# Attention's scores, a state space layer's matrices and skip, and the first unit of a stage, in another order

## The reference, cut to what matters

```python
for i in range(4):                    # attention, gating, state space, attention
    x = x + mixer_i(rmsnorm(x, norm_g[i, 0]))
    x = x + conv_gated_ffn(rmsnorm(x, norm_g[i, 1]), ...)
# attention: 16 heads of 64, instead of a softmax
z = q @ k.T / 8
log_1m = where(mask, log_sigmoid(-z), 0)
w = where(mask, exp(log_sigmoid(z) + cumsum_from_the_right(log_1m) - log_1m), 0)
o = (w @ v) @ w_o
# state space
bbar_re = coef_re * b_re - coef_im * b_im ; bbar_im = coef_re * b_im + coef_im * b_re
y = C x (a complex scan over time of bbar u) + d_skip * u
out = glu(gelu(y) @ w_glu)
```

## Time and profile before

| | us |
|---|---|
| median of 3 runs | 1801.25 (1799.35 to 1802.07) |
| the profiled execution, as a whole | 1802.3 |
| its span, first to last instruction | 1800.5 |
| PE, DVE, ACT, POOL busy | 1689.0, 1238.5, 844.9, 156.1 |
| mean granted TensorE clock | 0.978 of 2.4 GHz |

### The profile page before, as it was taken

The page is one execution under the profiler, slowest core; times in us unless marked ns, Lnnn a source line. Parts: engine busy times, 40 slices in busy tenths (PEclk is TensorE's granted clock), DMA queues, the critical chain, the costliest instruction groups (busy, mean ns, idle before and its releaser), DMA issues.

```text
span 1800.5 us, 34542 instructions
## 1 busy us (share of the span) xinstructions
PE 1689.0 (94%) x14415; PEld 1600.2 (89%) x14429; DVE 1238.5 (69%) x1567; ACT 844.9 (47%) x964; POOL 156.1 (9%) x128
## 2 busy tenths in 40 slices
PE   6999999998899997799999999999999999989997
PEld 6979999898899985599999897999998658889997
DVE  5847777786887757867777784777776667555454
ACT  5355545546445441245555535555544633343343
POOL 1002000103920043100000100200000000000000
PEclk9999999899999989999999999999999999999999
DMA  7804545535345531353554680445452032044551
GB/s 297 333 13 164 178 181 183 188 133 187 141 173 177 186 118 72 142 209 142 183 184 182 230 334 19 167 173 188 175 187 94 24 117 94 25 156 174 185 184 70
DMA packets 40050, 286.50 MB, mean 159 GB/s; under 512 B 4576, under 2 KB 4576, under 8 KB 5664
## 3 DMA queue, kind: packets, MB, share of 16 engines
q1 hardware_dynamic: 39024, 280.99, 43.1%
q10 hardware_dynamic: 944, 4.33, 0.6%
HBM read 284.25 MB, written 1.05 MB: 158 GB/s over the span
## 4 chain that ended last, share of the span: by engine, by line
PE 65%; DVE 17%; ACT 9%; issue 6%; POOL 1%; DMA 1%; DVEq 0%; ACTq 0%; POOLq 0%; SPq 0%
PE PS L1770 19%; PE PS L1771 19%; PE PS L1772 19%; ACT whi L386 5%; DVE wlo L928 4%; DVE AR L1153 4%; ACT AR L498 1%; DVE AR L1264 1%; DVE AR L1261 1%; ACT AR L589 1%; ACT AR L591 1%; DVE XL L972 1%; PE PS L2374 1%; POOL AR L2533 1%; DVE AR L1139 1%
## 5 line engine op out<-in xcount | busy, mean ns | idle before, releaser
L1770 PE MATMUL PS<-XH,whi 128*128 128x256 f32 (+1 forms) x2696 | 787.6, 292 | 46.8 <-DVE wlo L928 35.0
L1771 PE MATMUL PS<-XL,whi 128*128 128x256 f32 (+1 forms) x2696 | 778.4, 289 | 0.0
L1772 PE MATMUL PS<-XH,wlo 128*128 128x256 f32 (+1 forms) x2696 | 778.0, 289 | 0.0
L928 DVE TENSOR_TENSOR wlo<-raw,whi 128x2048 fp32r<-128x2048 f32 x240 | 557.3, 2325 | 180.7 <-ACT whi L386 180.6
L1770 PEld LDWEIGHTS PS<-XH,whi 128*128 128x128 f32 x2696 | 522.0, 194 | 60.6 <-issue 29.5
L1771 PEld LDWEIGHTS PS<-XL,whi 128*128 128x128 f32 x2696 | 522.7, 194 | 4.4 <-issue 0.2
L1772 PEld LDWEIGHTS PS<-XH,wlo 128*128 128x128 f32 x2696 | 522.5, 194 | 4.2
L386 ACT ACTIVATE whi<-raw 128x2048 fp32r<-128x2048 f32 x240 | 456.0, 1902 | 72.4 <-PE PS L1772 47.9
L1770 PE MATMUL PS<-HH,whi 128*128 128x256 f32 x880 | 250.7, 285 | 13.0 <-DVE HL L1173 8.5
L1772 PE MATMUL PS<-HH,wlo 128*128 128x256 f32 x880 | 249.7, 284 | 0.0
L1771 PE MATMUL PS<-HL,whi 128*128 128x256 f32 x880 | 249.7, 284 | 0.0
(11 more groups left out here) (365 smaller groups left out, 1522.5 us busy)
## 6 DMA issues: line engine op xcount, KB each, us to landing
raw<-wst SPq DMA_DIRECT2D x248, 1024.0 KB, 4.8
AR<-mst SPq DMA_DIRECT2D x17, 1024.0 KB, 5.5
XT<-x_in SPq DMA_DIRECT2D x2, 512.0 KB, 6.2
AR<-crow ACTq DMA_DIRECT2D x2, 512.0 KB, 5.7
AR<-sbc ACTq DMA_DIRECT2D x1, 1024.0 KB, 5.8
AR<-ctxin ACTq DMA_DIRECT2D x1, 1024.0 KB, 5.6
y_out<-XT SPq DMA_DIRECT2D x1, 1024.0 KB, 3.9
AR<-sgw ACTq DMA_DIRECT2D x1, 512.0 KB, 3.6
```

Of the source, the lines that this page charges most:

```text
L928: dve.tensor_tensor(wlo[:, r, :], raw[:, u % RING, :], whi[:, r, :].bitcast(F32), ALU.subtract)\
L1770: pe.matmul(dst, sh, mh, start=first, stop=False, **kw)
L1771: pe.matmul(dst, sh, ml, start=False, stop=False, **kw)
L1772: return pe.matmul(dst, sl, mh, start=False, stop=last, **kw)
```

## The change

It has five parts.

1. *Attention.* PE computes the scores of pairs 0 and 1 ahead of its last unit of v, DVE bounds both and takes the first maximum, and ACT takes exp and log of both, ahead of that unit's results. Behind pair 7's scores PE puts the first unit of the output projection in pieces (`begin`): tiles 0 and 1, and 2 and 3, between the last steps.
2. *First units* of attention, gating and state space go by tiles: both halves of tile k, then tile k + 1, in a bank cleared with a product of zeros. The sum of squares stands behind the first unit instead of in it, the row in the second half of the second unit.
3. *Matrices.* Sixteen POOL products (eight of 64 x 512, eight of 128 x 512) leave `discretize`; DVE makes the matrices in the FFN before with fourteen instructions, four, four, three and three of them at four places between parts of its loop. POOL's memset of 2,048 columns moves to the start of `discretize`, and its coefficients come ahead of its copies.
4. *Skip.* ACT scales U5 by d in place, PE adds it to the bank with a product by the identity, and ACT takes the gelu from the bank. DVE's `outputs` is gone.
5. *State space steps.* At steps 1, 3 and 5 half of the modulation unit stands ahead of `inputs`, half behind.

The diff, cut:

```diff
@@ ScalarE, attention
                 for n in range(4):
                     ahead(t.u)
+                    if n == 3:
+                        act.preload_act_table_set("natural_log_exp_and_others")
+                        softplus(0)
+                        softplus(1)
                     used(t.u)
...
+                    if 2 <= p < 8:
+                        softplus(p)
@@ ScalarE, state_space
                 for b in range(4):
-                    act.wait_ge(S["y5_sum"], b + 1)
+                    act.wait_ge(S["y5_ready"], 2 * b + 1)
+                    for k in (2 * b, 2 * b + 1):
+                        a = act.activation(U5[:, k, :], U5[:, k, :], ACT.Copy, scale=vcol("ssm_d", k))
+                    a.then_inc(S["u5_skip"], 1)
+                    act.wait_ge(S["y5_ready"], 2 * b + 2)
                     y = U5[:, 2 * b:2 * b + 2, :]
-                    act.activation(y, y, ACT.Gelu_apprx_tanh).then_inc(S["gelu5"], 1)
+                    act.activation(y.rearrange("p k (c e) -> p k c e", e=2),
+                                   PS[:, 4 + b % 2, :].rearrange("p (k e c) -> p k c e", k=2, e=2), ACT.Gelu_apprx_tanh)\
+                        .then_inc(S["gelu5"], 1)
@@ VectorE, attention
                 for n in range(4):
+                    if n == 3:
+                        bounded(0)
+                        bounded(1)
                     ahead(t.u)
+                    if n == 3:
+                        maximum(0)
                     late_rows(late + 4 + n)
...
+                    if 2 <= p < 8:
+                        bounded(p)
+                    if 1 <= p < 8:
+                        maximum(p)
@@ VectorE, new (called as ffn(1, aside=matrices, then=4))
+            def matrices(p):
+                if p == 0:
+                    return
+                if p == 1:
+                    dve.wait_ge(S["s5_coef"], 1)
+                    dve.wait_ge(S["s5_in"], 16)
...
+                dve.tensor_tensor(first, b16(c0), v0, ALU.mult)
+                link(dve.tensor_tensor(BT, b16(c1), v1, ALU.mult))
+                if p < 3:
+                    for g in range(2):
+                        r = slice(64 * g, 64 * g + 64)
+                        ins = dve.tensor_tensor(XB[0][p - 1][r, :, 16 * g:16 * g + 16], first[r], BT[r], op)
+                    link(ins)
+                elif p == 3:
+                    link(dve.tensor_tensor(first, first, BT, op))
+                else:
+                    dve.tensor_tensor(first, first, BT, op).then_inc(S["s5_mats"], 1)
@@ VectorE, state_space
-                def outputs(b):
-                    dve.wait_ge(S["y5_ready"], 2 * b + 2)
-                    for kk in range(2):
...
-                        ins = dve.scalar_tensor_tensor(u5, u5, vcol("ssm_d", 2 * b + kk), y5, ALU.mult, ALU.add)
@@ TensorE, features (tokens has the same for its halves c)
+                if first and scales == 0:
+                    pe.matmul(PS[:, b, :], ZB[:, 0:P], ZB[:, :], start=True, stop=False, skip_group_check=True)
+                    for k in range(KT):
+                        operand(True, k, per)
+                        for m in range(2):
+                            mm = product(PS[:, b, m * T:(m + 1) * T], w(slot, k * 256 + m * P, k * 256 + m * P + P),
+                                         x(k, at, at + T), False, k == KT - 1, skip_group_check=True)
+                    mm.then_inc(S["w_used"], 1)
+                    scale_sums(0, 1, 3, (1, 0))
@@ TensorE, attention
                 for n in range(4):
+                    if n == 3:
+                        scores(0)
+                        scores(1)
                     tokens()
...
                 for p in range(10):
+                    if 2 <= p < 8:
+                        scores(p)
+                    if p >= 8:
+                        begin(range(2 * p - 16, 2 * p - 14), 1, T)
...
-                residual(1)
+                begin(range(4, KT), 1, T)
+                residual(1, 1)
@@ TensorE, state_space
+                    if c:
+                        pe.wait_ge(S["u5_skip"], b + 1)
+                        for kk in range(2):
+                            pe.matmul(bank[:, kk * T:(kk + 1) * T], ident,
+                                      U5[:, 2 * b + kk, :].rearrange("p (c e) -> p e c", e=2), start=False, stop=False, **kw)
...
                     if s % 2 and s < 7:
+                        modulation(s, 7, range(4))
                         inputs(s // 2 + 1)
-                    modulation(s, 7)
+                        modulation(s, 7, range(4, KT))
@@ GpSimd, discretize
-                    link(pool.tensor_tensor(BT, b16(c1), v1, ALU.mult))
...
+                pool.tensor_tensor(CFI, T0, DEN, ALU.mult).then_inc(S["s5_coef"], 1)
...
+                pool.wait_ge(S["s5_mats"], 1)
+                pool.memset(MG[:, :, 0:1], 0.0).then_inc(S["s5_set"], 1)
```

More of the change, by code:

```diff
@@ L124, in __init__ @@
         self.free = 0
+        self.rows = 0, 3
         self.bank = 0
@@ L1747, in _ @@
             gating(3)
-            ffn(1, then=4)
+            ffn(1, aside=matrices, then=4)
             state_space(5)
@@ L1830, in tokens @@
                 slot = unit_ready(t.u)
+                if first:
+                    pe.matmul(PS[:, b, :], ZB[:, 0:P], ZB[:, :], start=True, stop=False, skip_group_check=True)
+                    for k in range(KT):
+                        operand(True, k)
+                        for c in range(2):
+                            mm = product(PS[:, b, c * 256:(c + 1) * 256], x(k, c * P, (c + 1) * P),
+                                         w(slot, k * 256, (k + 1) * 256), False, k == KT - 1, skip_group_check=True)
+                    mm.then_inc(S["w_used"], 1)
+                    scale_sums(0, 1, 3, (1, 0))
+                    t.u += 1
+                    return
                 for c in range(2):
@@ L1903, in begin, with residual @@
                     t.u += 1
-            def residual(per):
-                for mp in range(4):
+            def residual(per, begun=0):
+                for mp in range(begun, 4):
                     if mp == 0 and per == 2:
@@ L1977, in attention, with scores @@
                     features(n == 0, scales=n)
+                n0 = t.att
+                kw = dict(skip_group_check=True)
+                pp = t.pp + 4
+                def scores(p):
+                    r = p % 3
+                    if p == 2:
+                        pe.wait_ge(S["pp_taken"], pp)
+                    if p >= 3:
+                        pe.wait_ge(S["wb_ready"], n0 + p - 2)
+                    for i in range(2):
+                        b = PS[:, 2 * r + i, :]
+                        pe.matmul(b[:, 0:P], IDB[:, :], MKB[:, :], start=True, stop=False, **kw)
+                        pe.matmul(b[:, 2 * P:3 * P], IDB[:, :], MKB[:, :], start=False, stop=False, **kw)
+                    for first, last, queries in ((0, P, slice(0, T)), (P, T, slice(P, T))):
+                        for i in range(2):
+                            rows = slice(64 * i, 64 * i + 64)
+                            o = 2 * first
+                            mm = pe.matmul(PS[:, 2 * r + i, o:o + T - first], QK[rows, KT + p, first:last],
+                                           QK[rows, p, queries], start=False, stop=True, **kw)
+                    mm.then_inc(S["sc_ready"], 1)
```

151 lines of the change are left out of this document (61 added, 90 removed).

## The result

The changed kernel takes 1788.9 us (median of 4 runs, 1787.18 to 1789.2); the kernel before, timed beside it, 1800.78 (4 runs). The ratio is 0.9934, 95% interval 0.9922 to 0.9946: 11.9 us gained, where 19.5 were forecast. The profiled execution took 1787.18 as a whole, with a span of 1785.4 and a mean clock of 0.981.

The account below looks back on a forecast made before the run. PE, busy 94% of the span, was taken to set the time. Gains of 6.2 + 7.3 + 2.7 + 3.1 + 0.2 = 19.5 us took 1802.3 to 1782.8 profiled, about 1782 median; range 1775.5 to 1791.

Parts of the forecast that it names:

- Attention: Both attentions: early scores and projection pieces fill PE's waits at start and end; 6.2 us gained in the first, 7.3 second.
- First units: First units of attention, gating and state space, done by tiles: 2.7 us gained in all, ends set by PE's clock.
- the gating term: Gating's first unit by tiles: 0.7 us gained, between 1.9 at full clock and −0.35 with the clock low as before.
- Matrices: Second FFN, after gating: 7.8 us of PE gaps and clock can go, 4.7 of DVE's added work shows; 3.1 gained.
- So DVE's slack at such a place is 0.75 to 1.1 us: Second FFN, DVE's four matrix groups: this slack hides part of their 9.4 us, so 1.8, 1.5, 0.95 and 0.8 show.
- The steps: State space steps with skip on PE and split modulation: gains 3.4, losses 1.6, 0.9 and about 0.7; 0.2 us gained.
- 1.7 us later three times: State space steps: `inputs` behind four modulation tiles comes later; DVE waits about 2.1 us at one or two of them.
- it loses 4 x 0.86 = 3.4 us of `outputs`: State space steps: DVE sets the pace, so removing its four `outputs` of 0.86 us gains 3.4 us.
- B: Rival, less gain: all 9.4 us of DVE's matrices show and the state space steps lose 1.5; 1788 us, chance 0.15.
- A: Rival, more gain: clock stays up in first units (6.6), only 3.8 of matrices shown, 2 from skip; 1775.5 us, chance 0.20.
- D: Rival, slower than before: PE falls to its lower clock behind each new wait ahead of sums; 1812 us, chance 0.04.
- C: Rival, attention gains by half only: early exp, log and bounds do not fit under v's last unit; 1791 to 1793, chance 0.09.

Follow-up runs that it names:

- the doubled groups: The changed kernel with each of DVE's four groups of matrix instructions in the second FFN repeated; 1798.0 us.
- the loads held back: SP delays loads replacing modulation units until the small matmuls are through: 1776.1 us with skip on PE, last identity early, inputs first; 1780.08 with both step parts undone.

## Why the prediction was right in part, and which term failed

**Attention: right, mechanism and size.** The list of PE from the end of v's last unit to the end of the projection's first was summed to 35.6 us; it takes 35.33, without a gap. What moved is visible in the timeline of the changed kernel, PE and DVE:

```profile
93.46 0.70 PE L2079 MATMUL PS<-AR,CST 128*128 128x256 f32 x2
93.58 0.96 DVE L1264 TENSOR_SCALAR AR<-PS 128x768 f32<-128x768 f32 x1 [1.23 <-PE PS L2057]
113.82 0.95 DVE L1264 TENSOR_SCALAR AR<-PS 128x768 f32<-128x768 f32 x1
```

Pair 2's bound comes at 93.58 (forecast 93.3, 98.46), pair 7's five steps of 4.05 us later. The middle is as it was, the two ends are gone. The second attention gained 7.6 with its first unit, since its low stretch went too (a clock of 1.00 in the pairs now, .91 in the earlier trace rows). Other kernels with the same attention and first units gain 6.0 to 9.1 there, by the clock of the first unit: over the 15 us from POOL's last sum it is 1.00 where 9.1 are gained, .89 where it is 7.6, as here, and .77 where it is 6.0.

**First units: a wash.** The new wait ahead of the sums is there, 2.02 us in gating, where 2.2 were worked out:

```profile
349.22 1.05 PE L1907 MATMUL PS<-CST,AR 128*128 128x1 f32 x8 [2.02 <-POOL AR L2597]
```

The gain was 0.45 and 2.0 us against the trace of before, for 0.7 and 1.9 forecast. But the run with the old order shows that this agreement is partly luck: the base of the gating term was the clock of one execution. The term should have been written as about −0.4 for gating, with the clock as a separate chance. The time gives no gain to this part at all.

**Matrices: right mechanism, both sides mis-sized.** The term was 3.1 and measured 6.7. The ends of PE's units tell the two sides apart, set beside those of the FFN after the first attention, which has the same matmuls and whose unit ends agree to 0.02 us in both traces. In the kernel before the second FFN fell back by 9.5 us. In the changed kernel it is 0.1 behind at the first group, 2.0 after it, 2.8 after the second, and stays there. So 9.4 could go where the prediction had 7.8: the rest, which it expected to stay with POOL's copies and coefficients, went too. And DVE's groups cost 2.7 where it had 4.7: 1.9, 0.8, 0.1 and nothing. 7.8 − 4.7 became 9.4 − 2.7.

The cost hardly shows as gaps, since PE falls back by some 0.6 us at each of several waits of 0.37. The count of records does show it: the same 20 us of the stage, from 56 us behind POOL's last sum, in the first FFN (no group) and in the second (behind its first group), both at full clock:

```profile
201.74:221.74 20.00, 20.00 (x169) 20.00 (x168) 15.53 (x21) 9.08 (x11) 0.00 (x0) 1.00 0.51 183
485.54:505.54 20.00, 18.93 (x154) 18.33 (x153) 16.36 (x20) 9.94 (x12) 0.00 (x0) 1.00 0.47 172
...
490.02 0.39 PE L1807 MATMUL PS<-HH,whi 128*128 128x256 f32 x1 [0.32 <-DVE wlo L940]
496.41 0.39 PE L1807 MATMUL PS<-XH,whi 128*128 128x256 f32 x1 [0.37 <-DVE wlo L940]
502.80 0.39 PE L1807 MATMUL PS<-XH,whi 128*128 128x256 f32 x1 [0.37 <-DVE wlo L940]
```

The step that failed is "So DVE's slack at such a place is 0.75 to 1.1 us", taken for all four places from one gap of 0.37 in another FFN. It held at the first place (0.8); at the others the slack is about twice as large (1.7 to 2.3, by the doubled groups). Why the first has less is not shown.

**The steps: wrong, and most of the missing gain.** The forecast had 0.2 us gained with −3 as its low end; 7.7 were lost. Three steps failed.
- "1.7 us later three times", of which DVE was to wait "at one or two of them": the half unit ran at half clock at step 1 (a stretch of 3.1 us at .60), since PE had waited 6.14 us for POOL there, and the delay came at all three steps: 2.9, 1.9 and 1.3 us more waiting than before. This was in reach: the same wait and a clock of .66 behind it (690 to 700 us) stand in the trace of before. But only at step 2 is the wait the half unit's own. Against the kernels that differ in it alone, the halves add 2.2 and 2.9 us there (2.73 against 0.56 with the skip on DVE, 3.46 against 0.59 on PE) and take waiting away at steps 4 and 6 (1.43 and 0.0 against 1.68 and 0.57; 2.53 and 1.43 against 4.65 and 4.67), where they shorten PE's stalls; at those two steps the missing `outputs` and the stalls make the rest.
- "it loses 4 x 0.86 = 3.4 us of `outputs`": ahead of steps 4 and 6 PE's chain was the later one, so what DVE saved in steps 2 and 4 became waiting (1.43 and 0.0 us with `outputs` on DVE, 2.53 and 1.43 without). Only the cut in step 6, behind which no `inputs` follow, and the one at the very end could count.
- The last step was priced at 0.9 for the identity and 0.7 of clock. It took 2.08 for the identity, 0.94 of waiting for ACT (nothing in the sum asked what stood ahead of the scaling in ACT's list) and over 1 more for the last outputs at half clock: from its first piece to the next, PE needed 9.27 us instead of 5.02.

Under these lay what no sum had: PE's stalls for its own instructions. In the kernel before they are 2.42 and 2.13 us and almost covered by DVE. Every edit that moved the modulation units' end against the small matmuls changed them, to 2.27 and 1.10, to 3.97 and 3.91, to 0.44 once. That is why undoing part 5 alone made the kernel no faster: its waits at steps 4 and 6 are the longest of all. With the loads held back, part 4 is worth 4.6 us in the steps (−5.0 against −0.4) where its last identity product is early.

**The time.** 1788.9 lies 7 us above the forecast and inside the range. The rivals: B's gap (the steps lose) came, but of the matrices 2.7 us showed instead of 9.4, even less than A's 3.8; D's clock fell behind new waits, but cost more than before only in the steps; C is excluded by the full row of attention. On D the prediction said that no low stretch stands behind a wait of 1 to 3 us in the middle of dense work. None as long as that of gating does, but a shorter one is in the trace of before, behind the wait of 2.84 us at 509.60:

```profile
510.40:513.80 3.40, 3.40 (x19) 3.40 (x17) 1.46 (x4) 2.41 (x3) 0.00 (x0) 0.51 0.84 306
```

So the 19.5 of the forecast became 15.1 between the two traces by errors that partly cancel: 7.9 us less in the steps, 3.6 more in the second FFN. That the total lay inside the range owes something to this. The other 3.2 us down to 11.9 are the two profiled executions' distance from their medians.

What stays open: what sets the moment of the packet and the 2.2 to 2.6 us from its start to PE's next matmul, which are there with free queues too and leave stalls of 0.6 to 1.5 us; and what decides whether gating's first unit runs at .50 or 1.00 with the same code.

## What to carry to other kernels

Work that is put ahead of a step "since PE is idle there" is priced at the clock that the idle time leaves behind, and every engine that hands over to it has a list of its own: ask what stands ahead in each. A gap put down to issue in a dense stretch of tiny matmuls is a wait like any other; look at which DMAs run then, and let the large loads start behind such a stretch if their buffers aren't needed soon. And before a gap in one trace is counted as gain, look whether the same code shows it twice.

## What the runs showed of the hardware

- Instructions are fetched during the run: the page counts 63 packets (1.03 MB) on an instruction queue, 16 KB each, eleven of them in the steps of the kernel before (682 to 761 us). That they are PE's is inferred: in all 27 stalls of the 14 traces PE went on 2.2 to 2.6 us after the start of such a packet.

```profile
q8 instruction: 63, 1.03, 0.2%
```

  The Trainium skill, "Runtime: NRT & Kernel Launch", section "Instruction fetch mechanics", says that each engine's instructions come in blocks of 16 KiB through a queue of their own while the engine runs, and that crossing from one block to the next is mostly hidden. The trace agrees on the blocks. In the steps it is not hidden: PE stood up to 3.97 us, and the measurement decides.
- In the 19 stalls without held loads the packet started within 0.5 us of the end of a 1 MB weight transfer, and PE stood 0.4 to 4.0 us. With the transfer held back it stood 0.6 to 1.5. In each of the four pairs of kernels that differ in the holding alone, both stalls shrank, from 1.1 to 4.0 us down to that.
- The two identity products take 1.17 us at full clock and 2.08 at half, the last step's 128 records of 64 columns 1.98 and 3.47: these small matmuls slow down nearly as much (1.75 times) as the wide ones (1.78 times).
